# Product-key experts in a decoder step: U transposed two tiles ahead in three buffers, and the low part of the query weights made two blocks ahead

## The reference, cut to what matters

```python
q = (ht @ w_query).reshape(T, PEER_HEADS, 2, PEER_DQ // 2)
s = jnp.einsum('thpd,hpnd->thpn', q, sub_keys)
top_s, top_i = lax.top_k(s, PEER_TOPK)              # 16 of 128 keys, in 8 heads x 2 halves
cand_s = top_s[:, :, 0, :, None] + top_s[:, :, 1, None, :]
fin_s, pos = lax.top_k(cand_s, PEER_TOPK)           # 16 of the 256 pairs
gate = jax.nn.softmax(fin_s, axis=-1)
act = jax.nn.gelu(jnp.einsum('tkd,td->tk', expert_u[ik], xk))
return jnp.einsum('tk,tkd->td', gk * act, expert_v[ik])
```

## Time and profile before

| | |
|---|---|
| median of 3 runs | 3962.49 us (3962.09 to 3970.85) |
| profiled execution | 3964.46 us, its span 3962.4 us |
| PE busy in the span | 3388.7 us (86%), 17345 matmuls |
| DVE busy | 2587.2 us (65%) |
| ACT busy | 911.8 us (23%) |
| granted TensorE clock, mean | 0.911 of full |
| stage of the scores in the trace | about 945 to 1227 us |
| stage of the choice in the trace | about 1228 to 2029 us |

### The profile page before, as it was taken

One profiled execution on the slowest core, in us unless ns is written; L12 is line 12 of the kernel. 1 busy time (PEld: TensorE's weight loads), 2 busy tenths in 40 slices (PEclk: granted clock), 3 DMA queues, 4 the chain that ended last, 5 costly groups with the idle time before them and its releaser, 6 DMA issues. The chain is left out here.

```text
span 3962.4 us, 45328 instructions
## 1 busy us (share of the span) xinstructions
PE 3388.7 (86%) x17345; PEld 2907.8 (73%) x17345; DVE 2587.2 (65%) x5414; ACT 911.8 (23%) x1300; POOL 799.8 (20%) x628
## 2 busy tenths in 40 slices
PE   7994513995898888888889999999499999999997
PEld 5453313645888888888889999999488888888885
DVE  2006465113114777777768888888488888998996
ACT  2001000103111121121224444444222222222222
POOL 0000000000000010000013333333144444443441
PEclk8995556996998998998989999999799999999998
DMA  2100001122011333333348988888789988989994
GB/s 87 43 0 11 13 6 26 59 70 88 27 32 55 116 107 116 108 112 112 107 149 288 321 302 316 288 314 317 266 302 301 301 299 301 299 300 298 302 300 162
DMA packets 435375, 695.55 MB, mean 176 GB/s; under 512 B 239172, under 2 KB 293256, under 8 KB 429000
## 3 DMA queue, kind: packets, MB, share of 16 engines
q1 hardware_dynamic: 351016, 386.31, 29.3%
q0 software_dynamic: 84144, 306.35, 22.7%
HBM read 580.12 MB, written 110.64 MB: 174 GB/s over the span
## 5 line engine op out<-in xcount | busy, mean ns | idle before, releaser
L1747 POOL DMA_INDIRECT dr_row<-in_peer_v_dram,idx x288 | 424.8, 1475 | 661.5 <-DVE acc_s L1766 654.3
L1747 POOL DMA_INDIRECT gr_row<-in_peer_u_dram,idx x240 | 290.4, 1210 | 466.3 <-DVE raw L1756 444.1
L1766 DVE SCALAR_TENSOR_TENSOR acc_s<-dr_row,gate,acc_s 128x1024 f32<-128x1024 f32 x288 | 367.3, 1275 | 0.0
L2272 DVE TENSOR_TENSOR acc<-pd_po,acc 128x512 f32<-128x512 f32 x384 | 264.3, 688 | 117.2 <-PE pd_po L2305 117.2
L1756 DVE CUSTOM_DVE_ANT_0 gr_row<-gr_row,xs 128x1024 f32<-128x1024 f32 x240 | 288.6, 1217 | 0.0
L2162 ACT ACTIVATE pg_wb<-pg_pw 128x512 f32<-128x512 f32 x192 | 210.8, 1099 | 56.4 <-PE pg_pw L2140 56.3
L2119 DVE TENSOR_SCALAR pg_hot_i<-pg_iota,sel_t 128x128 f32<-128x128 f32 x768 | 213.2, 357 | 0.0
L1725 ACT ACTIVATE ta_a<-ta_pa 128x384 f32<-128x384 f32 x128 | 62.8, 491 | 634.2 <-PE ta_pa L1710 634.2
L2140 PE MATMUL pg_pw<-pg_hot_i,pg_hot_j 128*128 128x128 f32 x1536 | 204.0, 276 | 3.0 <-DVE pg_hot_i L2119 3.0
L2140 PEld LDWEIGHTS pg_pw<-pg_hot_i,pg_hot_j 128*128 128x128 f32 x1536 | 195.4, 193 | 3.4 <-DVE pg_hot_i L2119 3.4
L1747 POOL DMA_INDIRECT tr_row<-in_peer_u_dram,idx x48 | 57.7, 1203 | 676.3 <-DVE raw L1756 585.1
(11 more groups left out here) (488 smaller groups left out, 8208.3 us busy)
## 6 DMA issues: line engine op xcount, KB each, us to landing
pd_v<-in_peer_v_dram SPq DMA_DIRECT2D x128, 512.0 KB, 6.6
w_d<-pg_wb SPq DMA_DIRECT2D x48, 1024.0 KB, 9.5
pd_w<-w_d SPq DMA_DIRECT2D x128, 384.0 KB, 5.7
pd_a<-act_d SPq DMA_DIRECT2D x128, 384.0 KB, 6.2
ta_u<-in_peer_u_dram SPq DMA_DIRECT2D x64, 512.0 KB, 3.6
ga_u<-in_peer_u_dram SPq DMA_DIRECT2D x64, 512.0 KB, 6.8
act_d<-ta_a SPq DMA_DIRECT2D x128, 192.0 KB, 1.9
act_d<-ga_a SPq DMA_DIRECT2D x128, 192.0 KB, 4.3
```

Source lines behind the costliest of these rows:

```text
L1747: pool.indirect_dma_start(self.buf[i % self.n][:], None, self.table, bass.IndirectOffsetOnAxis(ap=self.idx[:, col:col + 1], axis=0)).then_ ...
L1766: self.nc.vector.scalar_tensor_tensor(out=out, in0=self.buf[i % self.n][:], scalar=w[:, col:col + 1], in1=out, op0=ALU.mult, op1=ALU.add). ...
L2272: nc.vector.tensor_tensor(out, po[(OUTS * g + o) % NPO][:], out, ALU.add).then_inc(o_added, 1)
```

## The change

Two parts.

In the stage of the scores, DVE makes the low part of block c + 2 at the head of round c, ahead of the copies of `score(c)`, where it made block c + 1 there before.

In the stage of the choice, `Up` gets a number of buffers for the transposed U: three here, and two as before in the stage of the gates. Tiles 0 and 1 are transposed and split ahead of the loop; in round n, PE transposes tile n + 2, ACT makes its high parts, and DVE its low parts at the same points of the choice as before. The gathered rows of this stage get two buffers in place of four. SP's list is as it was: `load` of tile n + 2 stands behind `keep` of the first half of tile n, and `u_sb` has two buffers.

```diff
             low(1)
             for c in range(NU):
-                if c >= 1 and c + 1 < NU:
-                    low(c + 1)
+                if c + 2 < NU:
+                    low(c + 2)
                 for b in range(3):
                     dve.wait_ge(s_done, 3 * c + b + 1)
...
-        self.ut = [[sb(f"ut{b}{x}", [P, KD, P], F32R) for x in "hl"] for b in range(2)]
+        self.ut = [[sb(f"ut{b}{x}", [P, KD, P], F32R) for x in "hl"] for b in range(buffers)]
+        self.nb = buffers
...
     def high(self, act, n, half):
-        if n >= 2:
-            act.wait_ge(self.a_done, 2 * (n - 1))
+        if n >= self.nb:
+            act.wait_ge(self.a_done, 2 * (n - self.nb + 1))
         act.wait_ge(self.turned, 2 * n + half + 1)
...
-    return 14 * q + 14 * (point + 1) // POINTS
+    return min(2 * (UP_TOPK - 2), 14 * q + 14 * (point + 1) // POINTS)
...
-        up = Up(ctx, nc, "ta", 0, u_d, act_d, h)
-        rows_u = Rows(ctx, nc, "tr", u_d, idx, 0, ROWS_TOPK, 4)
+        up = Up(ctx, nc, "ta", 0, u_d, act_d, h, 3)
+        rows_u = Rows(ctx, nc, "tr", u_d, idx, 0, ROWS_TOPK, 2)
...
-            for half in range(2):
-                up.high(act, 0, half)
+            for n in range(2):
+                for half in range(2):
+                    up.high(act, n, half)
...
                 up.gelu(act, n, 0)
-                if n + 1 < UP_TOPK:
-                    up.high(act, n + 1, 0)
-                    up.high(act, n + 1, 1)
+                if n + 2 < UP_TOPK:
+                    up.high(act, n + 2, 0)
+                    up.high(act, n + 2, 1)
                 up.gelu(act, n, 1)
...
-            for half in range(2):
-                up.turn(pe, 0, half)
+            for n in range(2):
+                for half in range(2):
+                    up.turn(pe, n, half)
             for n in range(UP_TOPK):
                 up.up(pe, n, 0)
-                if n + 1 < UP_TOPK:
-                    up.turn(pe, n + 1, 0)
-                    up.turn(pe, n + 1, 1)
+                if n + 2 < UP_TOPK:
+                    up.turn(pe, n + 2, 0)
+                    up.turn(pe, n + 2, 1)
                 up.up(pe, n, 1)
...
-            for half in range(2):
-                up.low(dve, 0, half)
+            for n in range(2):
+                for half in range(2):
+                    up.low(dve, n, half)
...
                     for m in range(lows_by(q, point - 1), lows_by(q, point)):
-                        up.low(dve, 1 + m // 2, m % 2)
+                        up.low(dve, 2 + m // 2, m % 2)
...
-        up = Up(ctx, nc, "ga", UP_TOPK, u_d, act_d, h)
+        up = Up(ctx, nc, "ga", UP_TOPK, u_d, act_d, h, 2)
```

More of the change, by code:

```diff
@@ L1653, with __init__ @@
 class Up:
-    def __init__(self, ctx, nc, tag, base, u_d, act_d, h):
+    def __init__(self, ctx, nc, tag, base, u_d, act_d, h, buffers):
         def sb(name, shape, dt=F32):
@@ L1709, in up @@
         for i, (x, y, k) in enumerate(steps):
-            mm = self.nc.tensor.matmul(self.pa[c][:, 0:WB], self.ut[n % 2][x][:, k, :], self.h[y][:, k, c * WB:(c + 1) * WB],
+            mm = self.nc.tensor.matmul(self.pa[c][:, 0:WB], self.ut[n % self.nb][x][:, k, :], self.h[y][:, k, c * WB:(c + 1) * WB],
                                        start=(i == 0), stop=(i == len(steps) - 1))
@@ L1714, in high @@
     def high(self, act, n, half):
-        if n >= 2:
-            act.wait_ge(self.a_done, 2 * (n - 1))
+        if n >= self.nb:
+            act.wait_ge(self.a_done, 2 * (n - self.nb + 1))
         act.wait_ge(self.turned, 2 * n + half + 1)
-        self.nc.scalar.activation(self.ut[n % 2][0][:, 4 * half:4 * half + 4, :],
+        self.nc.scalar.activation(self.ut[n % self.nb][0][:, 4 * half:4 * half + 4, :],
                                   self.pt[half][:].rearrange("p (k s) -> p k s", k=4), ACT.Copy).then_inc(self.ut_hi, 1)
@@ L1729, in low @@
         dve.wait_ge(self.ut_hi, 2 * n + half + 1)
-        self.nc.vector.tensor_tensor(self.ut[n % 2][1][:, k, :], self.pt[half][:].rearrange("p (k s) -> p k s", k=4),
-                                     self.ut[n % 2][0][:, k, :].bitcast(F32), ALU.subtract).then_inc(self.ut_lo, 1)
+        self.nc.vector.tensor_tensor(self.ut[n % self.nb][1][:, k, :], self.pt[half][:].rearrange("p (k s) -> p k s", k=4),
+                                     self.ut[n % self.nb][0][:, k, :].bitcast(F32), ALU.subtract).then_inc(self.ut_lo, 1)
 class Rows:
```

## The result

| | before | changed |
|---|---|---|
| median | 3962.29 us (4 runs, 3957.94 to 3970.85) | 4161.07 us (4 runs, 4155.36 to 4166.34) |
| span of the profiled execution | 3962.4 us | 4153.2 us |
| stage of the scores | 280.2 us | 233.0 us |
| stage of the choice | 805.0 us | 1046.8 us |
| mean granted clock | 0.911 | 0.892 |

The changed kernel takes 1.0504 times as long (95% interval 1.0487 to 1.0520). A stage is read here from its first load to the first load of the next one: the scores from 947.35 to 1227.54 before and from 946.61 to 1179.61 now, the choice from there to 2032.51 before and to 2226.36 now. So the scores gained 47.2 us, the choice lost 241.8, all stages behind it gained 3.1 and those ahead 0.7: together the 190.8 us between the two spans.

A forecast was written before the change was run, and what follows sets the result against it. It took PE and DVE waiting for each other, neither full, to bound the stage of the choice. Choice +205.5 and scores -44.7 gave +160.8 on 3964.46, so 4125.3, as a median 4123 us; range 4078 to 4172.

The forecast's parts named there:

- rival 2: Stage of the choice: each wait costs 2.5 us of clock, or loads land at 4.3; 4165 to 4175 us; 16 in 100.
- The load's latency on PE: Stage of the choice: PE stands 4.9 us for U's load in each of 62 tiles, 303.8 us in all.
- The clock behind each wait: Stage of the choice: slow matmuls behind each load wait lose 1.7 us, 62 times, 105.4 us (62 to 155).
- What goes in return: Stage of the choice: PE's old waits for DVE's low parts, 126.3 us, and their 78 us of clock disappear.
- The start of the stage: Stage of the choice: tile 1's transposes, now ahead of the first `up`, wait for tile 0's low parts, 0.6 us.
- Two buffers for rows: Stage of the choice: two buffers for gathered rows in place of four cost nothing, or 10 us if dots stand close.
- The scores: Stage of the scores: 25.6 us of waits and 19.1 us of clock go, -44.7 us together.
- The sum: Whole kernel: choice +205.5 and scores -44.7 us, together +160.8 us against the profiled 3964.46 us.
- the hidden load: Stage of the choice: the load is hidden and PE and DVE come apart; -224 us, so 3739 us; 4 in 100.
- The third: Stage of the choice: waits cost less, loads land at 3.3, clock loses 1.0 to 1.4; about 4075 us; 14 in 100.
- The fourth: The two stages cancel, the load's wait being partly hidden; change near zero, 3950 to 3975 us; 2 in 100.

The follow-up runs named there:

- the early loads: The changed kernel with SP loading tiles 0 to 3 ahead of the loop, then tile n + 4 behind `keep` of tile n's first half: 3729.25 us.
- the filled waits: The changed kernel with unread matmuls added in each of 62 tiles between `up`'s first half and `turn`: 4050.0 us with 24, 4064.92 us with 12.
- the early loads alone: The kernel before with the scores' part and U loaded a tile earlier, transposed U still in two buffers and one tile ahead: 3921.21 us, 0.9892.
- the run with 12 added matmuls: The changed kernel with 12 unread matmuls added in each of 62 tiles between the first half of `up` and `turn`: 4064.92 us.

## Why the prediction was right, and where it was off

It said 4123 us within 4078 to 4172, slower; it is 4161. The mechanism was right. The size was less so: 4161 lies above the forecast's own range (4095 to 4150), and within the whole range only because that took in the lower end of rival 2.

- **The load's latency on PE** (303.8 us): 313.9, 5.06 us a wait in place of 4.9. Shown by the waits, and by the early loads, which take it away. It is 10 us of the error. The two steps were sized rightly: in 61 of the 62 tiles the load is issued 1.23 to 1.25 us after PE is free, it lands a median 3.6 us later, and the median wait is 4.87 us. What was missing is nine waits of 5.9 to 7.0 us: in one of them the load was issued late, in eight it landed late, and why is open. The estimate of 3.2 us by the fit of the Trainium skill, "DMA: Bandwidth & Descriptors", section "Anatomy of one DMA", was not met; that section gives the fit for transfers issued from GpSimd, and this one is issued from SP.
- **The clock behind each wait** (1.7 us, 105.4 in all): 132 us, 2.1 a wait, and 27 us of the error. This is the term that was mis-sized. Of 1.7 behind 3.21 us and 2.5 behind 4.00 I took the lower, although the waits to come were longer than both, on the ground that what is slow while PE stands costs nothing. That ground is true, but it did not make up for the length: a granted clock of 0.81 over 1035.2 us is worth 197 us, of which PE lost 132, so some 65 fell on its standing. That the cost comes from PE's standing is shown by the filled waits.
- **What goes in return** (126.3 + 78 us): gone, as the waits of the changed kernel show. Its split between waits and clock was read wrongly. By PEld, which shows when the next instruction could have started, the old waits are 143.5 us, 2.6 each:

```profile
PEld ta_pa L1710 <- DVE ta_ut0l L1730: 72.3, 28, 3.5
PEld ta_pa L1710 <- DVE ta_ut1l L1730: 71.2, 27, 3.5
```

  That leaves 794.2 - 590 - 143.5 = 61 us for the clock, 1.1 a wait. The clock's own record says so too: 0.91 granted over 794.2 us leaves room for about 71 us, and not for 78. The sum of the two, 204, is the same, so for the old waits it makes no difference. For the new ones it does: their 4.9 us were counted from a weight load's start (1620.27), by PEld, but the 1.7 us behind each by PE's rows. By PEld the two rows are 1.4 lost behind 3.53 us of waiting and 2.3 behind 4.24, and the measured 2.1 behind 5.06 is close to the second. A 1.4 on the right ruler would have put the forecast 19 us lower and further off: the mixture helped by luck.
- **The start of the stage** (0.6): from its first load to the first `up` 7.8 us, before 7.0, so 0.8. Right.
- **Two buffers for rows** (nothing): right, by the run that changes only them.
- **The scores** (-44.7): -47.2 between the stages' starts, -45.3 alone. A block at full clock without a wait is 13.84 us and not the 13.91 that I had from 15.74 - 1.83, so the 14 waits were 1.9 us each; 14 x 1.90 + 12 x 1.59 = 45.7. Two readings were off without effect: the block that starts at 1054.57 is block 6 and not 4, and block c's matmuls end 16 us before block c + 2 starts, 1.2 blocks and not a block and a half.
- **The sum**: choice +205.5 forecast, +241.8 measured, 36 us too little. The scores gained 2.5 us more than forecast and the untouched stages 3.8, so the spans miss by 30 us (+160.8 against +190.8). The medians, which differ by 198.8 us, miss by 38; the 8 us between the two are within the spread of the runs (11 us for the changed kernel).
- **The rivals.** The second was the nearest: it gave about 4175 by 2.5 us of clock a wait, or 4165 by loads that land at 4.3, and the measured 2.1 us and 4161 lie between the forecast and it. The first, the hidden load, didn't happen here, and gave 3739 us as its price; the run in which the loads are early took 3729. The third needed loads that land at 3.3 us and a clock that costs 1.0 to 1.4 a wait; the median load took 3.6 and the clock cost 2.1. The fourth needed a wait of 2.3 us, and the shortest was 4.66.

The signs named beforehand came out so: 63 waits, 298.6 us by the row of PE (about 300 was said); the stage 1035 us (1000); PE busy 741 of 1035, 72% (69); clock 0.81 (0.85); DVE's waits 438 us (390); a block of the scores 13.84 us (13.9); the end of the scores at 1179.6 (1183).

## What to carry to other kernels

A buffer further ahead at one step of a pipeline moves the need of every step before it. Here the transposes moved one tile ahead and the loads that feed them did not, so a transfer that had a tile of time was waited for whole; before adding a buffer, list for each input of the moved step who issues it and behind which wait, and move that as well. On top of the scores' part, whose kernel was at 0.9888 of the time before, the third buffer and the transposes a tile further ahead alone led to 1.0504, the early loads alone to 0.9892, and both together to 0.9428.

When a trace shows two engines each waiting for the other, add up what each has of its own: 590 us of PE and 606 of DVE in a stage of 794 said what a decoupled stage could reach, and it reached 609.

## What the runs showed of the hardware

- Behind waits of 5.06 us on average, the eight transposes and some of the matmuls behind them run at TensorE's lower level, in all 62 tiles, and a wait costs 2.1 us on top of itself; behind 1.22 us on average it costs nothing that can be told. So 62 waits for a load, 314 us in all, cost 446. With 1488 matmuls that nobody reads put into the waits, the kernel was 111 us faster.
- The Trainium skill, "TensorE: Matmul & The Clock Gate", section "HAM oscillation", describes just this: a wait for a transfer in each tile, and each tile starting at the half clock. This trace agrees: the clock of the stage went to 0.81 with such a wait in each tile, and to 1.00 without.
- In the run with 12 added matmuls, waits of 3.08 us on average cost 0.5 us each, about half of the 1.1 us that waits of 2.6 us cost in the kernel before. The length of a wait alone doesn't say what it costs.
